# Cross-attention in units of two query blocks, value products two rounds behind, and the second layer's output projection begun among the last units

## The reference, cut to what matters

```python
def cross_attention(h, mem_n, wq, wkv, wo):
    q = (h @ wq).reshape(B, S, X_HEADS, X_HEAD_DIM)            # S = 512, 4 heads, head dim 256
    kv = (mem_n @ wkv).reshape(B, M, 2, X_HEADS, X_HEAD_DIM)   # M = 256
    s = jnp.einsum('bshd,bmhd->bhsm', q, kv[:, :, 0]).astype(jnp.float32) * X_HEAD_DIM ** -0.5
    p = jax.nn.softmax(s, axis=-1)
    o = jnp.einsum('bhsm,bmhd->bshd', p.astype(h.dtype), kv[:, :, 1]).reshape(B, S, D_MODEL)
    return o @ wo
```

## Time and profile before

| | us |
|---|---|
| median of 3 runs (2393.1, 2398.16, 2398.38) | 2398.16 |
| the profiled execution | 2392.53 |
| its span in the trace | 2390.7 |
| PE busy (97% of the span) | 2326.1 |
| DVE busy (58%) | 1381.5 |
| ACT busy (36%) | 858.1 |

### The profile page before, as it was taken

The page is one execution under the profiler, slowest core; times in us unless marked ns, Lnnn a source line. Parts: engine busy times, 40 slices in busy tenths (PEclk is TensorE's granted clock), DMA queues, the critical chain, the costliest instruction groups (busy, mean ns, idle before and its releaser), DMA issues.

```text
span 2390.7 us, 28766 instructions
## 1 busy us (share of the span) xinstructions
PE 2326.1 (97%) x11510; PEld 1875.6 (78%) x11510; DVE 1381.5 (58%) x2466; ACT 858.1 (36%) x1483; POOL 153.4 (6%) x101
## 2 busy tenths in 40 slices
PE   8999999998999999998999999999999989999997
PEld 6677778877777787877788888888888878888886
DVE  5967565559665656587545544444755545444444
ACT  4333443342344434254424433233322334332232
POOL 0514000006210000020000000000000000000000
PEclk9999999999999999999999999999999999999998
DMA  4222222321222223323223232232223212232221
GB/s 161 70 67 68 83 73 90 98 80 53 76 75 74 81 93 97 105 81 107 97 90 115 96 97 93 92 97 97 91 95 97 88 36 88 97 97 97 90 96 53
DMA packets 61289, 211.22 MB, mean 88 GB/s; under 512 B 7103, under 2 KB 8383, under 8 KB 61028
## 3 DMA queue, kind: packets, MB, share of 16 engines
q1 hardware_dynamic: 61156, 209.39, 27.0%
HBM read 207.25 MB, written 2.11 MB: 88 GB/s over the span
## 4 chain that ended last, share of the span: by engine, by line
PE 88%; DVE 10%; ACT 1%; issue 1%; DMA 0%; DVEq 0%; SPq 0%; ACTq 0%
PE ps L324 25%; PE ps L326 25%; PE ps L325 25%; PE ps L612 3%; PE ps L524 3%; DVE t_wlo L171 2%; PE ps L587 1%; PE ps L349 1%; PE ps L350 1%; PE ps L351 1%; DVE t_Tb L177 1%; DVE t_Tb L174 1%; PE ps L413 1%; DVE t_QKV L165 1%; DVE t_ST L538 1%
## 5 line engine op out<-in xcount | busy, mean ns | idle before, releaser
L324 PE MATMUL ps<-t_P0H,t_whi 128*128 128x512 f32 x1664 | 678.5, 408 | 9.5 <-DVE t_P0L L174 9.3
L326 PE MATMUL ps<-t_P0H,t_wlo 128*128 128x512 f32 x1664 | 657.8, 395 | 0.0
L325 PE MATMUL ps<-t_P0L,t_whi 128*128 128x512 f32 x1664 | 656.5, 395 | 0.0
L180 ACT ACTIVATE t_whi<-t_raw 128x1024 fp32r<-128x1024 f32 (+2 forms) x396 | 405.1, 1027 | 373.0 <-PE ps L326 321.5
L171 DVE TENSOR_TENSOR t_wlo<-t_raw,t_whi 128x1024 fp32r<-128x1024 f32 (+2 forms) x396 | 491.2, 1243 | 11.4 <-ACT t_whi L180 6.3
L324 PEld LDWEIGHTS ps<-t_P0H,t_whi 128*128 128x128 f32 x1664 | 314.7, 189 | 103.4 <-issue 24.7
L326 PEld LDWEIGHTS ps<-t_P0H,t_wlo 128*128 128x128 f32 x1664 | 313.8, 189 | 73.4
L325 PEld LDWEIGHTS ps<-t_P0L,t_whi 128*128 128x128 f32 x1664 | 314.5, 189 | 67.8 <-issue 2.2
L324 PE MATMUL ps<-t_P1H,t_whi 128*128 128x512 f32 x900 | 354.7, 394 | 0.7 <-DVE t_P1L L171 0.7
L326 PE MATMUL ps<-t_P1H,t_wlo 128*128 128x512 f32 x900 | 354.8, 394 | 0.0
L325 PE MATMUL ps<-t_P1L,t_whi 128*128 128x512 f32 x900 | 354.2, 394 | 0.0
(11 more groups left out here) (237 smaller groups left out, 2699.8 us busy)
## 6 DMA issues: line engine op xcount, KB each, us to landing
t_raw<-in_wts SPq DMA_DIRECT2D x364, 512.0 KB, 3.4
t_raw<-in_wts SPq DMA_DIRECT2D x16, 384.0 KB, 3.0
t_raw<-in_wts SPq DMA_DIRECT2D x4, 520.0 KB, 6.4
t_X<-in_xT SPq DMA_DIRECT2D x4, 512.0 KB, 7.1
t_raw<-in_wts SPq DMA_DIRECT2D x8, 256.0 KB, 2.6
outT<-t_X SPq DMA_DIRECT2D x8, 256.0 KB, 2.3
t_E<-in_memT SPq DMA_DIRECT2D x1, 1024.0 KB, 5.1
t_E<-scr SPq DMA_DIRECT2D x4, 256.0 KB, 3.9
```

The lines of the kernel that those rows point to most:

```text
L180: return lambda e: e.activation(o, a, f, **k)
L324: e.matmul(bank[:, 0:N], wh, xh, start=first, stop=False)
L325: e.matmul(bank[:, 0:N], wh, xl, start=False, stop=False)
L326: return e.matmul(bank[:, 0:N], wl, xh, start=False, stop=end)
```

## The change: what it does

The two layers' cross-attention gets code of its own in `cross`, and the kind "plain" leaves `attention`.

- A unit is now two query blocks: 8 units. Per unit one S of 4 score matmuls into one bank, one maximum over 2 x 256, two exponentials, one reciprocal and one broadcast multiply, a T of 4 transposes with one copy of 128 x 512, and a V of 4 matmuls with 256 columns.
- Round i emits N(i-1), S(i), fill, V(i-2), T(i-1), fill. The transposes of a unit and its values are separated by both portions of fill and the next scores.
- Rates: 5 per yield in layer 0, 13/3 in layer 1. Since there are 20 yields in place of 36, part of `kv(1)` is now run after the last unit.
- In layer 1, behind the query tiles, the first two tiles of `wo` are opened side by side, and their input tiles 0 to 5 are taken as fill: tiles 0 to 3 of both, then 4 and 5 of both. Their input tiles 6 and 7 and the other six tiles follow after the last unit.
- `kv` looks at units `2h` and `2h+1` where it looked at `4h` to `4h+3`.

```diff
@@ in kv (the same for "over")
-            while before and not all("T" in u for u in before[4 * h:4 * h + 4]):
+            while before and not all("T" in u for u in before[2 * h:2 * h + 2]):
@@ in cross
-        un = []
-        for h in range(4):
-            for i in range(4):
-                un.append(dict(
-                    kind="plain", len=256, pair=h, nout=2, first=i == 0, last=i == 3,
...
+        un = [dict(head=h, half=n) for h in range(4) for n in range(2)]
...
+        def scores(u):
...
+                for a in range(2):
+                    q0 = 128 * (2 * u["half"] + a)
+                    for d in range(2):
+                        i = e.matmul(bank[:, 256 * a:256 * a + 256], qX[:, 2 * h + d, q0:q0 + 128],
+                                     KT[:, 2 * h + d, :], start=d == 0, stop=d == 1)
...
+            o = op(DV, lambda e: e.reduce_max(s[:, 0:2], both(bank), axis=AX), p, sfree)
+            o = op(DV, ts(s[:, 2:4], s[:, 0:2], -1.0, None, ALU.mult), o)
+            u["exp"] = [op(AC, act(t[:, 256 * a:256 * a + 256], bank[:, 256 * a:256 * a + 256], ACT.Exp,
+                                   bias=s[:, 2 + a:3 + a], accum_out=s[:, 4 + a:5 + a]), o, tfree)
+                        for a in range(2)]
...
+        def norm(u):
+            t, s = u["t"], u["s"]
+            r = op(DV, lambda e: e.reciprocal(s[:, 6:8], s[:, 4:6]), u["exp"])
+            u["P"] = op(DV, mult(both(t), both(t), s[:, 6:8].unsqueeze(2).broadcast_to([128, 2, 256])), r)
...
+        def values(u):
...
+                for d in range(2):
+                    o = held[h][d][0][:, 256 * n:256 * n + 256]
+                    for j in range(2):
+                        c = 256 * h + 128 * d
+                        i = e.matmul(o, VM[:, j, c:c + 128], pt[:, 256 * j:256 * j + 256], start=j == 0, stop=j == 1)
...
+            if n == 1:
+                for d in range(2):
+                    m, bank = 2 * h + d, held[h][d][0]
+                    a = op(AC, act(P1.hi[:, m, :], bank, ACT.Copy), p)
+                    o = op(DV, sub(P1.lo[:, m, :], bank, P1.hi[:, m, :].bitcast(F32)), a)
...
+        def main():
+            n = len(un)
+            for i in range(n + 2):
+                if 1 <= i <= n:
+                    norm(un[i - 1])
+                if i < n:
+                    scores(un[i])
+                yield
+                flush()
+                if i >= 2:
+                    values(un[i - 2])
+                if 1 <= i <= n:
+                    turn(un[i - 1])
+                yield
...
         def fill():
             for h in range(1, 4):
                 yield from qs(h)
             if l == 0:
                 yield from kv(1, un)
+                return
+            for _ in range(3):
+                yield
+            for m in range(2):
+                open_.append(wo(m))
+            for parts, rest in ((range(0, 4), 1), (range(4, 6), 3)):
+                for g in open_:
+                    for k in parts:
+                        assert P1.tok[k] is not None
+                        next(g)
+                        for _ in range(1 + rest):
+                            yield
 
         if l == 0:
-            drive(attention(un, done), fill(), 5, 1)
+            drive(main(), fill(), 5, 1)
         else:
-            drive(attention(un, done), fill(), 9, 4)
-        run(mixed("xattn_wo", l, halves(0), 1.0, gname, P1))
+            drive(main(), fill(), 13, 3)
+        for g in open_:
+            run(g)
+        for m in range(len(open_), 8):
+            run(wo(m))
```

More of the change, by code:

```diff
@@ L531, in scores @@
                 mx, nm, l, es = (s[:, c:c + 1] for c in range(4))
-                if u["kind"] == "plain":
-                    o = op(DV, lambda e, mx=mx, bank=bank: e.reduce_max(mx, bank[:, 0:kl], axis=AX), p, sfree)
-                elif u["kind"] == "forget":
+                if u["kind"] == "forget":
                     a = op(DV, stt(t[:, 0:kl], bank[:, 0:kl], u["cq"][j], u["bias"][j], ALU.add, ALU.subtract),
@@ L548, in scores @@
                     o = op(DV, ts(nm, mx, -1.0, None, ALU.mult), o)
[L549 to L553, removed]
+                x = op(AC, act(t[:, 0:kl], t[:, 0:kl], ACT.Exp, bias=nm, accum_out=l), o)
                 if u["kind"] == "sink":
@@ L1231, in kv @@
                 yield from gemm_fm(MEM, w, parts8(), evac, N=256)
-            while before and not all("over" in u for u in before[4 * h:4 * h + 4]):
+            while before and not all("over" in u for u in before[2 * h:2 * h + 2]):
                 yield
@@ L1311, in cross @@
         run(qs(0))
-        un = []
-        for h in range(4):
-            for i in range(4):
-                un.append(dict(
-                    kind="plain", len=256, pair=h, nout=2, first=i == 0, last=i == 3,
[L1317 to L1332, removed]
+        un = [dict(head=h, half=n) for h in range(4) for n in range(2)]
+        def both(ap):
+            return ap.rearrange("p (a b) -> p a b", a=2)
@@ new lines, in scores, with f @@
+        def scores(u):
+            h = u["head"]
+            bank, free = SB.take()
+            t, tfree = TB.take()
+            s, sfree = STT.take()
+            def f(e):
+                for a in range(2):
[3 more added lines that the diff above has]
+                                     KT[:, 2 * h + d, :], start=d == 0, stop=d == 1)
+                return i
+            p = op(PE, f, [tok[2 * h], tok[2 * h + 1], kvt[("k", 2 * h)], kvt[("k", 2 * h + 1)]], free)
+            o = op(DV, lambda e: e.reduce_max(s[:, 0:2], both(bank), axis=AX), p, sfree)
[3 more added lines that the diff above has]
+                        for a in range(2)]
+            SB.give(bank, u["exp"])
+            u["t"], u["s"], u["T"] = t, s, True
@@ new lines, in norm, with turn, f @@
+        def norm(u):
+            t, s = u["t"], u["s"]
+            r = op(DV, lambda e: e.reciprocal(s[:, 6:8], s[:, 4:6]), u["exp"])
+            u["P"] = op(DV, mult(both(t), both(t), s[:, 6:8].unsqueeze(2).broadcast_to([128, 2, 256])), r)
+            STT.give(s, u["P"])
+        def turn(u):
+            t = u["t"]
+            bank, free = PTP.take()
+            def f(e):
+                for j in range(2):
+                    for a in range(2):
+                        i = e.transpose(bank[:, 256 * j + 128 * a:256 * j + 128 * a + 128],
+                                        t[:, 256 * a + 128 * j:256 * a + 128 * j + 128], ident[:, :])
+                return i
+            p = op(PE, f, u["P"], free, c_I)
+            TB.give(t, p)
+            pt, pfree = PTS.take()
+            u["PT"] = pt, op(AC, act(pt, bank, ACT.Copy), p, pfree)
+            PTP.give(bank, u["PT"][1])
@@ new lines, in cross, with f @@
+        held = {}
+        P1.tok = [None] * 8
+        def values(u):
+            h, n = u["head"], u["half"]
+            pt, ready = u["PT"]
+            if n == 0:
+                held[h] = [OB.take() for _ in range(2)]
+            def f(e):
+                for d in range(2):
+                    o = held[h][d][0][:, 256 * n:256 * n + 256]
+                    for j in range(2):
+                        c = 256 * h + 128 * d
+                        i = e.matmul(o, VM[:, j, c:c + 128], pt[:, 256 * j:256 * j + 256], start=j == 0, stop=j == 1)
+                return i
+            p = op(PE, f, ready, kvt[("v", 2 * h)], kvt[("v", 2 * h + 1)],
+                   [x[1] for x in held[h]] if n == 0 else None)
+            PTS.give(pt, p)
+            u["over"] = True
+            if n == 1:
[3 more added lines that the diff above has]
+                    o = op(DV, sub(P1.lo[:, m, :], bank, P1.hi[:, m, :].bitcast(F32)), a)
+                    P1.tok[m] = [a, o]
+                    OB.give(bank, o)
@@ new lines, in main, with nxt @@
+        def main():
[12 more added lines that the diff above has]
+                yield
+        def nxt(m, o):
+            norm_tile(m, o, gname, P0, sqa)
+        ev = residual(1.0, nxt, P0)
@@ L1334, in fill, with wo @@
+        def wo(m):
+            w = Weight(chunk("xattn_wo", l, halves(0), halves(128 * m, 1)))
+            return gemm_fm(P1, w, parts8(), ev(m))
+        open_ = []
         def fill():
```

## The result

| | before | changed |
|---|---|---|
| median, 4 runs each (us) | 2396.58 (2393.1 to 2398.38) | 2384.07 (2382.72 to 2385.27) |
| the profiled execution | 2392.53 | 2385.27 |
| its span | 2390.7 | 2383.5 |
| first stage (layer 0): L487 to L487 | 171.25 | 167.28 |
| second stage (layer 1): L487 to L487 | 132.26 | 125.30 |

The ratio is 0.995, 95% interval 0.9937 to 0.9963: 12.5 us less. The forecast was 2387.5, with a range from 2379 to 2394.

What follows compares the result with a forecast made beforehand. PE bounds the kernel (88% of the span). Layer 1 -9.7 + 3.25 - 0.3 = -6.7 and layer 0 -3.6 - 0.3 = -3.9 give -10.6 us, from the median 2398.16 to 2387.5; range 2379 to 2394.

Steps and rivals of the forecast that it cites:

- scores of head 1: Layer 1, round 2: PE waits for query tile 3, which ends one step before these scores; 0.25 us.
- scores of head 3: Layer 1, round 6: PE waits for the query tile, behind head 1's two `P1L` on DVE; 1.05 us.
- `wo` input tile 4: Layer 1, behind V of head 2: PE waits for the tile's `P1L` output; 0.35 to 0.4 us.
- `wo` tiles 6 and 7: Layer 1, straight behind the last values: PE waits for their output; 1.6 us.
- wide values, per layer: Values of 256 columns in both layers, priced by columns: V 1.74 for 1.78 us, 0.3 us saved per layer.
- Gaps, 9.7 and 3.6: PE idle between transposes and values, all taken as gone: 9.7 us at layer 1's end, 3.6 us in layer 0.
- A sign that came: Layer 0's unbroken stretch after the last values: PE waits for `whi` or `wlo` would prove the prediction wrong; none expected.
- rival 2: Wide values cost by instruction, not columns: up to 7.1 us further gain per layer, 2373; chance 0.05.
- Rival 1: Layer 1's new waits cost 7.0 us for 3.25, a `wlo` ahead on DVE; 2391.3; chance 0.17.
- Rival 3: Layer 0's unbroken stretch fed weights too slowly: 23 us more, 2411; chance 0.05.
- Rival 4: Waits only move elsewhere in the same chain, needing 7 us more of waits; 2398; chance 0.01.
- the gain of 13: Hitch-free case for both layers, subtracted from the runs' lower level 2393.1 to give 2380 for the range's lower end.

Runs made afterwards that it cites:

- experiment 6: Changed kernel with values first in each round, two query steps ahead of the first scores, third `wo` tile opened behind the last values: 2382.06 us, 0.9946.
- experiment 7: Changed kernel with values first in each round, two query steps ahead of the first scores, layer 1 rate 4 for 13/3: 2380.72 us, 0.9938.
- experiment 5: Changed kernel with each value matmul of 256 columns split into two of 128: 2383.65 us, ratio 0.9951.
- experiment 1: Kernel before, units of one block, no early `wo`, only values of unit i-2 moved behind the scores of unit i and fill: 2385.43 us, 0.9956.
- experiment 2: Changed kernel with the old order within a round (values of unit i-2 before scores of unit i), early `wo` kept: 2380.02 us, 0.9932.
- experiment 9: Changed kernel itself, unaltered, timed again beside experiment 7: 2384.03 us, ratio 0.9958.
- experiment 4: Changed kernel with the old order within a round and no `wo` among layer 1's units, leaving units of two blocks: 2386.18 us, 0.9959.
- experiment 8: Kernel of experiment 2, unaltered, timed again beside experiment 7: 2380.88 us, ratio 0.9946.
- experiment 3: Changed kernel without `wo` among layer 1's units, the fill ending after the query tiles, new order kept: 2386.3 us, 0.9959.

## Why the prediction was right, point by point

**The bound** was read rightly: the gain is PE's idle time in two short stretches, 10.93 by the stages for a forecast 10.6. It was not all that there was to have: the wait of 0.78 of the first scores in each layer, which the prediction does not name, was in both kernels, and experiments 6 and 7 removed it.

| term | forecast | measured (waits: listed) |
|---|---|---|
| layer 1, waits left: scores of head 1 | 0.25 | 0.19 |
| scores of head 3 | 1.05 | 0.77 |
| `wo` input tile 4 | 0.35 to 0.4 | 0.29 |
| `wo` tiles 6 and 7 | 1.6 | 1.41 |
| last V | 0 | 0 |
| wide values, per layer | 0.3 | 0.45 (experiment 5) |
| layer 0, new waits | 0, with up to 2 | 0.25 |
| layer 1 in all | -6.7 | -6.96 |
| layer 0 in all | -3.9 | -3.97 |

**Gaps, 9.7 and 3.6.** The count by starts of rows, and not by the list of waits (8.3 and 2.7), was the right one: with the listed waits and the same terms the sum would be -8.35 for both layers. Experiment 1 shows the 3.6 by itself.

**Waits left.** All four stand where the new order put them. As listed they come to 2.66 for a forecast 3.25, but the prices were distances between starts, and a wait costs more than its listed length. Worked back from the layer's total, 9.7 - 6.96 + 0.45, they cost 3.2, as priced. In layer 0 the terms give -3.6 - 0.45 + 0.25 = -3.8 for a measured -3.97.

**A sign that came.** The prediction called itself wrong if a wait for `whi` or `wlo` appeared in the unbroken stretch of layer 0. One did, of 0.25 us. Its size is within the 2 us that were allowed for hitches, but the statement that there would be none, PE busy throughout, did not hold to the letter. Its last 198 matmuls took 24.10 us from 1281.72 to 1305.82, for some 23.

**What makes the gap** was told incompletely: "a T, then nothing until ACT has copied" leaves out the maximum and the exponential of the next unit, which stand ahead of that copy and are 0.9 of each 1.36 (the maximum is named for the longest gap alone). The length was right all the same, since it was taken from rows and not worked out from the pieces.

**What takes the gap away** was put loosely: the steps of `wo` between, "and a unit's V no longer follows its T directly", as if both were needed. Experiment 1 (units of one block) and experiment 2 (units of two) show that either takes nearly all of it, and that in layer 1 the lag on top of the early `wo` is a loss. The number did not depend on it, the advice that one would draw from it does.

**Wide values by columns.** A wide V takes 1220.27 - 1218.55 = 1.72 us in the changed kernel's timeline, forecast 1.74:

```profile
1218.55 1.89 PE L1371 MATMUL ps<-t_PTb,t_VM 128*128 128x256 f32 x8
1220.27 0.60 PE L1347 MATMUL ps<-t_ident,t_Tb 128*128 128x128 f32 x4
```

That is 0.215 per record, against 0.111 for half the columns, so rival 2 fell. By the spacing that the Trainium skill gives (TensorE: Matmul & The Clock Gate, Back-to-back issue gap) experiment 5 would have lost 5.7 us per layer, an estimate; it lost 0.45, and the measurement decides.

**Rivals.** Rival 1 (7.0 us of waits, a `wlo` ahead of each tile) fell: 2.66. Rival 3 (the stretch of layer 0 is starved of weights) fell: one wait of 0.25, and the stretch carried 162 GB/s, against 113 in the earlier trace rows, with PE busy for 25.87 of 26.12 us. Rival 4 (nothing changes) fell. One bound of the range, the gain of 13, is not derived: without any wait left the prediction's own terms give 9.7 + 3.6 + 0.6 = 13.9.

**The whole time.** The medians moved by 12.5, the stages by 10.93. No stage accounts for the 1.6 between. The unchanged code ahead of the stages alone took 3.8 us longer in one of the two profiled executions, and in experiment 9 the same kernel lay 10.1 under the kernel before (2384.03 against 2394.14, its median there). I took the 10.6 from the median of three, 2398.16, which lay 1.6 over that of four; the other way round, from 2396.58, it would have been 2386.0. The remaining 1.6 between stages and medians is within what single executions of one kernel differ by, and no run explains it further.

## What to carry to other kernels

Where an engine waits for a round trip through another one, put its own work between, as much as the round trip takes. Count it with everything that stands ahead in the other engines' rows: here 0.85 us from two transposes to the values with nothing ahead, but 2.61 from the scores to the values where maximum and exponential of the next unit stand ahead; for units of two blocks 1.29 and 4.41 (experiment 4). Then look what the moved piece was covering where it stood: in this kernel the second cover for the same gap cost 2.4 us elsewhere. Price an order by the distances between starts of rows, and measure it between two marks that stand on both sides of the changed stretch. Tiles that are held open hold their weight buffers: here, with three such buffers, two open tiles cost nothing and a third made the tile behind wait 1.91 us, since nothing was prepared until it was done.

## What the runs showed of the hardware that was not expected

The two unchanged stretches between the marks repeat from one execution to another to some hundredths of a us. What differed lay ahead of the first mark, which stood between 1184.72 and 1188.52 in the eleven profiles. A part of it is the start (PE's first matmul at 9.32 us before, 10.24 in the changed kernel); another is the granted clock in one stretch of unchanged code, first of the kernel before, then of the changed one (the clock is the third number from the right):

```profile
1000.00:1180.00 180.00, 169.35 (x978) 138.42 (x978) 123.87 (x302) 77.84 (x150) 12.68 (x10) 1.00 0.29 95
```

```profile
1000.00:1180.00 180.00, 169.33 (x966) 138.83 (x965) 123.38 (x301) 77.73 (x151) 12.64 (x10) 0.98 0.28 92
```

The same code was granted 1.00, the upper level of 2.4 GHz throughout, in one execution and a mean of 0.98 in another. From PE's first matmul to the first mark pass 1175.40 and 1175.45 us in the two profiles with 1.00 in this stretch (the kernel before and experiment 1), 1176.63 to 1177.02 in the five with 0.99 (experiments 2, 5, 6, 8 and 9), and 1178.08 to 1178.42 in the four with 0.98 (the changed kernel, experiments 3, 4 and 7). So of the 3.80 us by which the first mark came later, 0.92 are the start, and the other 2.88 go with the clock. Experiment 9 is the changed kernel itself and had 0.99, so it is not the kernel that sets it. PE's gaps there are no place of the change, and what makes the clock differ from one execution to the next was not tried.
